# First attention of a two-block transformer kernel: rounds of two heads and two blocks of queries

## The chip, the cores and the metric

The kernel runs on one core of a Trainium2 chip. The metric is the device time of one execution in microseconds (us), as the median of several runs. TensorE multiplies matrices, VectorE (DVE in the profile) and ScalarE (ACT) work elementwise, GpSimd (POOL) does further elementwise work, and SyncE (SP) issues most transfers. Each engine works through its own instructions in program order, and semaphores tie the engines together.

## The reference

The program computes two transformer blocks one after the other, on 2048 tokens of 1024 features, all in float32. The change touches the attention of the first block alone:

```python
q = (rms_norm(x_q, q_norm_g) @ w_uq).reshape(B, S, 4, 192)      # 4 heads: 128 features and 64 rotary ones
q_nope, q_rope = q[..., :128], apply_rope(q[..., 128:], cos, sin)
k_nope, v = split((rms_norm(x_kv, kv_norm_g) @ w_ukv).reshape(B, S, 4, 256))
def attend(qn, qr, pq):                                          # for each block of 128 queries
    s = (einsum('bqhd,bkhd->bhqk', qn, k_nope) + einsum('bqhr,bkr->bhqk', qr, k_rope)) * 192 ** -0.5
    mask = pq[:, None, :, None] >= positions[:, None, None, :]
    p = softmax(where(mask, s, neg), axis=-1)
    return einsum('bqhk,bkhd->bqhd', p, v)
y_a = attend(...) * silu(gate_a)
```

The mask compares positions that are data, so every block of queries is multiplied with all 2048 keys. The cosines and sines of the rotary part are computed from the positions too. What follows (a pooling branch, the output product with a layer norm, and the whole second block with sparse attention and a gated recurrence) is not touched.

## The kernel before

**Groups and units.** Tokens are worked in G = 4 groups of TB = 512, each of BG = 4 blocks of P = 128 queries. The keys and values of all groups are made first. Then each group g makes its queries, runs the first attention and the output product ("1out", `project_out`), and the next group starts. `mla_units(g)` lists 16 units of the attention, a unit u being one head h of one block i: the four heads of a block, then the next block. `mla_steps(g)` is the order in which TensorE and VectorE go through the steps of the units. It is written out by hand, and each engine takes its own part of each step from it.

**A unit.** Its 128 queries are cut into four pieces of QUAD = 32, and the keys into 16 blocks of 128, each of four quarters. The step "score" (lines 2490 to 2506) writes four PSUM banks, one for each piece r: 16 products of 32 queries with 512 keys from `q_nope`, then 16 from `q_rope`. In a bank each 32 partitions hold the same queries with other keys. VectorE adds the mask, takes the maximum and writes `probs_1[n % 2]` (line 1862, four instructions), combines the maxima to biases (`bias_of`, lines 1741 to 1747), and writes one quarter of the next block's mask (`mask_of`, line 1733). ScalarE takes the four exponentials in place, with their sums (line 1430). In the step "turn" VectorE transposes them in squares of 32 (line 1876, four instructions) into `turned_1`, which is a view of `lat`, the buffer of the queries' latents. It waits before it until the value product of the unit before has been done (`pv_done`). In the step "value" TensorE multiplies 16 blocks of values (128 keys by 128 features) with `turned_1[:, k, :]`, 128 moving columns each, and adds up in a quarter of the bank `o_acc[i % 2]`.

**The order around it.** TensorE runs score(u), then value(u - 1). Once per block come "sums" (a small product that adds up the sums of the exponentials, line 2521, then a reciprocal), "share" (a product that spreads the reciprocals over the features, line 2527) and "blend" (VectorE multiplies with the gate and with `o_acc` into `y_all`, lines 1894 and 1898, and counts `y1_made`). Scores, sums and shares claim six banks in turn (`claim`, `drains`).

**Beside it.** GpSimd adds pairs of weight tiles and stores them during the attention of groups 0 and 1 (lines 1174 to 1177), and adds up parts of `y_all` once two of a group's four blends are done (`y1_made` at `BG * g + 2`). The positions of the keys lie as float32 in `pos_k`, which `rope_args` reads ahead of each group's queries (line 1667). After it ScalarE computes the tables (line 1295). Every f32 product shows as two MATMUL and two LDWEIGHTS records in the profile.

## Time and profile before

| what | value |
|---|---|
| runs: median (lowest to highest) | 3543.56 us (3541.99 to 3544.79) |
| the profiled execution: its time | 3533.97 us |
| its span, first to last instruction | 3532.0 us |
| mean granted TensorE clock | 0.969 |
| busy in the span: TensorE, VectorE, ScalarE, GpSimd | 94%, 59%, 38%, 20% |
| value products of the first attention (L2514) | 2048 records, 251.7 us busy |
| score products (L2497 and L2504) | 4096 records, 233.0 and 124.6 us busy |

A row of a group or of the timeline gives start and duration in us, engine, line, operation, what is written and read, the number of instructions (x32) and in brackets the idle time of the engine before them and what ended it. Matmuls overlap each other in a pipeline, so the time from one group's start to the next group's start says more than the durations. The granted clock is a share of TensorE's full 2.4 GHz, so 0.50 is its lower level of 1.2 GHz.

### The profile page before, as it was taken

What the parts mean: (1) busy time and instruction counts of PE and PEld (TensorE: products, weight loads), DVE (VectorE), ACT (ScalarE), POOL (GpSimd) and SP (SyncE); (2) the same over time, 40 slices, a digit from 0 to 9 for tenths busy, and PEclk for the clock granted to TensorE, in tenths of its full rate; (3) what the DMA queues carried; (4) which work ended last, traced back from release to release, by engine and by line L of the source; (5) the groups of instructions that cost most, each with busy time, mean ns of one, the idle gap of its engine ahead of it and who ended that gap; (6) DMA issues with size and microseconds to landing.
All of it is one profiled execution on the core that took longest, in us unless ns stands there. A gap on an engine that the chain in (4) does not pass through costs nothing.

```text
span 3532.0 us, 49781 instructions
## 1 busy us (share of the span) xinstructions
PE 3319.1 (94%) x18464; PEld 2044.8 (58%) x18464; DVE 2066.5 (59%) x4970; ACT 1358.4 (38%) x2595; POOL 706.4 (20%) x1093
## 2 busy tenths in 40 slices
PE   8999999999999999999989999899998898998887
PEld 3444577567656755745567455674555673545656
DVE  4417734773475457435563587835768635878653
ACT  2212312222222313132341465515775514786552
POOL 0016032112101210111121101312351111352011
PEclk9999999999999999989989999999999999998999
DMA  5226135304501420341204211041210041110004
GB/s 192 72 66 245 49 113 167 114 13 125 161 2 50 148 78 1 91 159 54 63 25 146 71 61 33 25 143 60 66 45 1 25 152 54 51 57 1 1 3 129
DMA packets 114159, 275.22 MB, mean 78 GB/s; under 512 B 11096, under 2 KB 12672, under 8 KB 111872
## 3 DMA queue, kind: packets, MB, share of 16 engines
q1 hardware_dynamic: 105584, 256.31, 22.8%
q10 hardware_dynamic: 8336, 15.74, 1.3%
q8 instruction: 148, 2.42, 0.3%
q14 instruction: 91, 0.75, 0.1%
HBM read 239.75 MB, written 32.26 MB: 77 GB/s over the span
## 4 chain that ended last, share of the span: by engine, by line
PE 78%; DVE 10%; ACT 6%; issue 5%; POOL 1%; DMA 0%; SPq 0%; ACTq 0%; DVEq 0%; POOLq 0%
PE bank L2342 24%; PE bank L2356 17%; PE o_acc L2514 6%; PE bank L2497 6%; PE bank L2744 3%; PE bank L2631 3%; PE bank L2504 3%; PE bank L2663 3%; PE bank L2756 2%; PE o_acc L2770 2%; PE bank L2593 1%; ACT prob_t L1485 1%; DVE tmp L2048 1%; PE bank L2415 1%; ACT index L1628 1%
## 5 line engine op out<-in xcount | busy, mean ns | idle before, releaser
L2342 PE MATMUL bank<-group_even,weights 128*128 128x512 f32 x1152 | 507.6, 598 | 11.2 <-DMA group_even<-in_x_t 5.8
L2342 PE MATMUL bank<-group_odd,weights 128*128 128x512 f32 x960 | 426.7, 600 | 6.2 <-ACT tmp L1471 6.2
L2342 PEld LDWEIGHTS bank<-group_even,weights 128*128 128x128 f32 x1152 | 218.4, 192 | 275.5 <-issue 275.3
L1430 ACT ACTIVATE probs<-probs,stat 128x512 f32<-128x512 f32 x256 | 181.7, 711 | 431.6 <-DVE stat L1747 431.6
L2342 PEld LDWEIGHTS bank<-group_odd,weights 128*128 128x128 f32 x960 | 181.9, 192 | 225.6 <-issue 225.2
L2514 PEld LDWEIGHTS o_acc<-lat,val 128*128 128x128 f32 x2048 | 242.2, 197 | 49.4 <-issue 41.4
L2514 PE MATMUL o_acc<-lat,val 128*128 128x128 f32 x2048 | 251.7, 283 | 12.9 <-DVE lat L1876 12.9
L2497 PE MATMUL bank<-k_nope,q_nope 128*32 128x512 f32 x2048 | 233.0, 595 | 0.0
L1862 DVE CUSTOM_DVE_ANT_0 probs<-bank,mask 128x512 f32<-128x512 f32 x256 | 161.4, 686 | 98.4 <-PE bank L2504 98.4
L2744 PE MATMUL bank<-kh,qa 64*128 64x512 f32 (+3 forms) x816 | 171.1, 501 | 16.0 <-DVE o_sb L2300 7.5
L1876 DVE STREAM_TRANSPOSE lat<-probs 128x512 f32<-128x512 f32 x256 | 168.8, 695 | 20.1 <-ACT probs L1430 20.0
L2356 PE MATMUL bank<-y_all,weights 128*128 128x256 f32 x768 | 172.4, 379 | 1.8 <-issue 1.8
L1619 ACT ACTIVATE prob_t<-bank 128x512 f32<-128x512 f32 (+3 forms) x240 | 116.6, 535 | 137.8 <-PE bank L2756 137.6
L2356 PEld LDWEIGHTS bank<-y_all,weights 128*128 128x128 f32 x768 | 145.6, 190 | 23.6 <-issue 4.1
L2770 PE MATMUL o_acc<-prob_t,v 128*64 128x128 f32 x1680 | 146.2, 282 | 10.7 <-ACT prob_t L1619 6.9
L2770 PEld LDWEIGHTS o_acc<-prob_t,v 128*64 128x64 f32 x1680 | 118.5, 139 | 56.7 <-issue 43.2
L2497 PEld LDWEIGHTS bank<-k_nope,q_nope 128*32 128x32 f32 x2048 | 60.0, 109 | 128.0 <-issue 118.2
L1144 POOL TENSOR_TENSOR y_all<-probs 128x512 f32<-128x512 f32 x32 | 33.4, 1045 | 492.5 <-DVE probs L1979 288.9
L2504 PE MATMUL bank<-k_rope,q_rope 64*32 64x512 f32 x2048 | 124.6, 595 | 0.0
L2744 PEld LDWEIGHTS bank<-kh,qa 64*128 64x128 f32 x816 | 79.2, 198 | 70.1 <-issue 38.7
L2048 DVE TENSOR_SCALAR_CACHE_REDUCE tmp<-index,mids 128x384 uint8<-128x384 f32 (+4 forms) x144 | 98.2, 719 | 11.1 <-POOL mids L1162 10.3
L2756 PE MATMUL bank<-ident,index 128*128 128x128 f32 x514 | 77.2, 292 | 23.7 <-ACT index L1628 21.6
(472 smaller groups left out, 6159.3 us busy)
## 6 DMA issues: line engine op xcount, KB each, us to landing
weights<-in_w_in SPq DMA_DIRECT2D x101, 512.0 KB, 3.6
weights<-w_sums SPq DMA_DIRECT2D x200, 256.0 KB, 3.3
weights<-in_w_out SPq DMA_DIRECT2D x96, 256.0 KB, 3.7
weights<-in_w_in_q SPq DMA_DIRECT2D x28, 512.0 KB, 3.6
weights<-in_w_in_q SPq DMA_DIRECT2D x54, 256.0 KB, 3.3
w_sums<-group_odd SPq DMA_DIRECT2D x10, 1024.0 KB, 4.6
weights<-in_w_i SPq DMA_DIRECT2D x20, 512.0 KB, 3.6
group_odd<-in_x_t SPq DMA_DIRECT2D x8, 1024.0 KB, 8.5
```

The source lines that it names most:

```text
L1430: A_(p, p, ACT.Exp, scale=QK_DIM ** -0.5, bias=stat[:, 16 + PARTS * (n % 2) + r:17 + PARTS * (n % 2) + r], accum_out=sums_1[:, i % 2, PART ...
L1862: drains(V.tensor_tensor_reduce(out=probs_1[n % 2][:, r * TB:(r + 1) * TB], in0=bank("score", i, h, r)[:], in1=mask[:, i % 2, r * TB:(r + ...
L1876: V.transpose(turned_1[:, :, r * QUAD:(r + 1) * QUAD], probs_1[n % 2][:, r * TB:(r + 1) * TB].rearrange("p (k q) -> p k q", k=NB)).then_in ...
L2048: V.tensor_scalar(tested_dve[:, b, 0:n], index_of(BG * g + b)[:, 0:n], mids[:, b, r:r + 1], 0.0, ALU.is_ge, ALU.add, accum_out=counts[:, b ...
L2342: ins = M(bank(*name)[:], ring[n % SLOTS][:, k * P:(k + 1) * P], rhs[:, k, :], start=(k == 0), stop=(k == chunks - 1))
L2356: ins = M(bank(*name)[:, 0:HALF], ring[n % SLOTS][:, at % 2 * TB + k * P:at % 2 * TB + (k + 1) * P], of[:, k, :], start=(OPENED_BY[m] == m ...
L2497: M(bank("score", i, h, r)[c * QUAD:(c + 1) * QUAD, :].rearrange("p (k n) -> p k n", n=QUAD), q_nope[:, h, b * P + r * QUAD:b * P + (r + 1 ...
L2504: ins = M(bank("score", i, h, r)[c * QUAD:(c + 1) * QUAD, :].rearrange("p (k n) -> p k n", n=QUAD), q_rope[half, h, at:at + QUAD], keys[:, ...
L2514: ins = M(o_acc[i % 2][:, h * P:(h + 1) * P], val[:, k, h * P:(h + 1) * P], turned_1[:, k, :], start=(h == 0 and k == 0), stop=(h == H1 - ...
L2744: ins = M(bank("s2", i, 2 * p + e, c)[:, at:at + end - first], qa[rows, p, (i % BG) * P:(i % BG + 1) * P], kh[rows, a, p, first:end], star ...
L2756: ins = nc.tensor.transpose(bank("p2_t", i, h, c)[:, (k % BG) * P:(k % BG + 1) * P], probs_of(g, u, e)[:, k * P:(k + 1) * P], ident[:])
L2770: ins = M(o_acc[i % 2][e * DH2:(e + 1) * DH2, p * P:(p + 1) * P], v2[:, k, h * DH2:(h + 1) * DH2], prob_slots[2 * (m % 2) + e][:, (k % BG) ...
```

## The change

A round is now two heads of two blocks, ROUND = 4 units. `mla_units` goes through a pair of blocks head by head, so that two units in a row have the same head. The values of the two are multiplied at once: the transposes of both units fill one buffer `turned_` of 16 x 256 columns, and a "value" step is made after every second unit, with 256 moving columns for each block of values and half a bank of `o_acc`. The transposes of an even unit wait until the value product of the pair before has been done; those of an odd unit wait for no product. Sums, share and blend are made once per round, as often as before. The mask quarters of a whole block are written in one go, in the units 0, 7, 8 and 15 of a group.

`turned_` takes the place of `lat` and `pos_k`. As the first attention now overwrites the positions, ScalarE loads 512 of them into `o_sb` at the end of each group but the last, after the last blend, and VectorE converts them to float32 ahead of `rope_args`.

```diff
--- before.py
+++ after.py
@@ -67,24 +67,30 @@
 PARTS = P // QUAD
 
 
+
+
+ROUND = 4
+
+
 def mla_units(g):
 
-    return [(BG * g + b, h) for b in range(BG) for h in range(H1)]
+    return [(BG * g + 2 * pair + b, h) for pair in range(BG // 2) for h in range(H1) for b in range(2)]
 
 
 def mla_steps(g):
 
     units = mla_units(g)
     for u, (i, h) in enumerate(units):
+        r = BG * g + u // ROUND
         yield ("score", u)
-        if u > 0:
-            if h == 0:
-                yield ("sums", i - 1)
-            if h == 1 and i % BG > 0:
-                yield from [("share", i - 1), ("blend", i - 1)]
-            yield ("value", u - 1)
+        if u > 0 and u % 2 == 0:
+            if u % ROUND == 0:
+                yield ("sums", r - 1)
+            if u % ROUND == 2 and u > ROUND:
+                yield from [("share", r - 1), ("blend", r - 1)]
+            yield ("value", u // 2 - 1)
         yield ("turn", u)
-    yield from [("sums", i), ("value", u), ("share", i), ("blend", i)]
+    yield from [("sums", r), ("value", u // 2), ("share", r), ("blend", r)]
 
 
 def mla_tiles(g):
@@ -588,12 +594,14 @@
         val = alloc(one, "val", [P, NB, TB])
         q_nope = alloc(one, "q_nope", [P, H1, TB])
         q_rope = alloc(one, "q_rope", [P, H1, TB // 2])
-        lat = alloc(one, "lat", [P, 4, TB])
+        turned_ = alloc(one, "turned", [P, NB, 2 * P])
+        lat = turned_[:, 0:NB // 2, :].rearrange("p k q -> p (k q)").rearrange("p (j t) -> p j t", j=4)
+        pos_k = turned_[:, NB // 2:, :].rearrange("p k q -> p (k q)")
         turns = alloc(one, "turns", [P, 2, TB])
         cos, sin = turns[:, 0, :], turns[:, 1, :]
-        pos_k = alloc(one, "pos_k", [P, S])
         pos_i = probs[:, 0:S].bitcast(i32)
         pos_k4, pos_k4_i = prob_t[:, 2, :], probs[:, S:S + TB].bitcast(i32)
+        pos_g = o_sb[:].bitcast(i32)
         pos_q = alloc(one, "pos_q", [P, NB * PARTS])
         pos_qi = probs[:, S + TB:S + TB + NB * PARTS].bitcast(i32)
         same = alloc(one, "same", [P, P])
@@ -640,7 +648,6 @@
         decay = alloc(two, "decay", [P, 2, BG])
         two.close()
         probs_1 = probs[:, 0:S], probs[:, S:2 * S]
-        turned_1 = lat[:, :, :].rearrange("p j t -> p (j t)").rearrange("p (k q) -> p k q", k=NB)
         spread_1 = prob_t[:, 0, :].rearrange("p (n q) -> p n q", q=QUAD)
         sums_1 = stat[:, 32:64].rearrange("p (a n) -> p a n", a=2)
         mask_i = probs[:, S:S + KC * P].bitcast(i32)
@@ -772,6 +779,7 @@
         dve_step = sem("dve_step")
         pool_step = sem("pool_step")
         rope_arg = sem("rope_arg")
+        pos_here = sem("pos_here")
         rope_made = sem("rope_made")
         k_normed = sem("k_normed")
         q_normed = sem("q_normed")
@@ -1427,8 +1435,12 @@
                         act.wait_ge(row_max, PARTS * (n + 1))
                         for r in range(PARTS):
                             p = probs_1[n % 2][:, r * TB:(r + 1) * TB]
+                            at = PARTS * (u % ROUND) + r
                             A_(p, p, ACT.Exp, scale=QK_DIM ** -0.5, bias=stat[:, 16 + PARTS * (n % 2) + r:17 + PARTS * (n % 2) + r],
-                               accum_out=sums_1[:, i % 2, PARTS * h + r:PARTS * h + r + 1]).then_inc(probs_made, 1)
+                               accum_out=sums_1[:, u // ROUND % 2, at:at + 1]).then_inc(probs_made, 1)
+                if g + 1 < G:
+                    act.wait_ge(y1_made, BG * (g + 1))
+                    act.dma_start(pos_g, A["pos_k"][:, (g + 1) * TB:(g + 2) * TB].broadcast_to([P, TB])).then_inc(pos_here, 16)
 
             second_begins(act)
             act.wait_ge(t5_made, 1)
@@ -1664,7 +1676,12 @@
                     dve.wait_ge(rope_made, n)
                 ang, turn = tmp[:, 0, :], tmp[:, 1, :]
                 fr = VEC["inv_freq"]
-                step(dve, V.tensor_scalar(ang, pos_k[:, g * TB:(g + 1) * TB], vec[:, fr:fr + 1], None, ALU.mult))
+                at = pos_k[:, g * TB:(g + 1) * TB]
+                if n > G:
+                    dve.wait_ge(pos_here, 16 * (n - G))
+                    step(dve, V.tensor_copy(ang, pos_g))
+                    at = ang
+                step(dve, V.tensor_scalar(ang, at, vec[:, fr:fr + 1], None, ALU.mult))
                 step(dve, V.tensor_scalar(turn, ang, 1.0 / TWO_PI, 12582912.0, ALU.mult, ALU.add))
                 step(dve, V.tensor_scalar(turn, turn, 12582912.0, None, ALU.subtract))
                 for c in (C1, C2, C3):
@@ -1710,7 +1727,7 @@
 
             dve.wait_ge(vec_here, 16)
             dve.wait_ge(const_here, 16 * 7)
-            step(dve, V.tensor_copy(pos_k[:], pos_i))
+            step(dve, V.tensor_copy(pos_k, pos_i))
             step(dve, V.tensor_copy(pos_q[:], pos_qi))
             step(dve, V.tensor_copy(pos_k4, pos_k4_i))
             for c in range(PARTS):
@@ -1754,7 +1771,7 @@
 
             def scale_queries(g):
 
-                V.tensor_tensor(lat[:], lat[:], wide(rstd, 4), ALU.mult).then_inc(q_normed, 1)
+                V.tensor_tensor(lat, lat, wide(rstd, 4), ALU.mult).then_inc(q_normed, 1)
 
             def pool_window(g, j):
 
@@ -1865,15 +1882,18 @@
                         for r in range(PARTS):
                             wait_drained(dve, "score", i, h, r)
                         bias_of(n)
-                        mask_of(i + 1, h)
+                        if u % (2 * ROUND) in (0, 2 * ROUND - 1):
+                            for r in range(PARTS):
+                                mask_of(i + 1, r)
                     elif kind == "turn":
                         u = st[1]
                         n = unit_no(g, u)
-                        if n > 0:
-                            dve.wait_ge(pv_done, n)
+                        if u % 2 == 0 and n > 0:
+                            dve.wait_ge(pv_done, n // 2)
                         for r in range(PARTS):
                             dve.wait_ge(probs_made, PARTS * n + r + 1)
-                            V.transpose(turned_1[:, :, r * QUAD:(r + 1) * QUAD],
+                            at = (u % 2) * P + r * QUAD
+                            V.transpose(turned_[:, :, at:at + QUAD],
                                         probs_1[n % 2][:, r * TB:(r + 1) * TB].rearrange("p (k q) -> p k q", k=NB)).then_inc(turned, 1)
                     elif kind == "sums":
                         i = st[1]
@@ -1888,14 +1908,15 @@
                                                op1=ALU.mult).then_inc(inverse_made, 1)
                     elif kind == "blend":
                         i = st[1]
-                        at = (i % BG) * P
+                        heads = slice(2 * (i % 2), 2 * (i % 2) + 2)
+                        tokens = slice(i % BG // 2 * 2 * P, (i % BG // 2 + 1) * 2 * P)
                         wait_tile(dve, "share1_t", i)
-                        share = o_sb[:].rearrange("p (h t) -> p h t", h=H1)
-                        drains(V.tensor_tensor(share, bank("share1_t", i)[:].rearrange("p (h t) -> p h t", h=H1),
-                                               gate[:, :, at:at + P], ALU.mult), "share1_t", i)
+                        share = o_sb[:].rearrange("p (h t) -> p h t", h=2)
+                        drains(V.tensor_tensor(share, bank("share1_t", i)[:].rearrange("p (h t) -> p h t", h=2),
+                                               gate[:, heads, tokens], ALU.mult), "share1_t", i)
                         wait_drained(dve, "share1_t", i)
-                        dve.wait_ge(pv_done, H1 * (i + 1))
-                        V.tensor_tensor(y_of(g)[:, 0:H1, at:at + P], o_acc[i % 2][:].rearrange("p (h t) -> p h t", h=H1), share,
+                        dve.wait_ge(pv_done, 2 * (i + 1))
+                        V.tensor_tensor(y_of(g)[:, heads, tokens], o_acc[i % 2][:].rearrange("p (h t) -> p h t", h=2), share,
                                         ALU.mult).then_inc(y1_made, 1)
 
                 late_sum("1", g, dve, V)
@@ -2505,14 +2526,15 @@
                                         q_rope[half, h, at:at + QUAD], keys[:, c], start=False, stop=True)
                             ins.then_inc(tile_ready, 1)
                     elif kind == "value":
-                        u = st[1]
-                        i, h = units[u]
-                        if h == 0 and i >= 2:
-                            pe.wait_ge(y1_made, i - 1)
+                        u = 2 * st[1] + 1
+                        h = units[u][1]
+                        r, e = BG * g + u // ROUND, u % ROUND // 2
+                        if e == 0 and r >= 2:
+                            pe.wait_ge(y1_made, r - 1)
                         pe.wait_ge(turned, PARTS * (unit_no(g, u) + 1))
                         for k in range(NB):
-                            ins = M(o_acc[i % 2][:, h * P:(h + 1) * P], val[:, k, h * P:(h + 1) * P], turned_1[:, k, :],
-                                    start=(h == 0 and k == 0), stop=(h == H1 - 1 and k == NB - 1), skip_group_check=True)
+                            ins = M(o_acc[r % 2][:, e * 2 * P:(e + 1) * 2 * P], val[:, k, h * P:(h + 1) * P], turned_[:, k, :],
+                                    start=(e == 0 and k == 0), stop=(e == 1 and k == NB - 1), skip_group_check=True)
                         ins.then_inc(pv_done, 1)
                     elif kind == "sums":
                         i = st[1]
```

## Rows read from the trace of the kernel before

**Rows 1.** The page's first part: busy time of each engine and share of the span

```profile
PE 3319.1 (94%) x18464; PEld 2044.8 (58%) x18464; DVE 2066.5 (59%) x4970; ACT 1358.4 (38%) x2595; POOL 706.4 (20%) x1093
```

**Rows 2.** Timeline of TensorE in group 2: start, duration in us, line, count

```profile
1056.38 3.84 PE L2514 MATMUL o_acc<-lat,val 128*128 128x128 f32 x32
1060.15 3.64 PE L2497 MATMUL bank<-k_nope,q_nope 128*32 128x512 f32 x32
...
1065.60 3.84 PE L2514 MATMUL o_acc<-lat,val 128*128 128x128 f32 x32
...
1074.82 0.40 PE L2521 MATMUL bank<-stat,same 128*128 128x16 f32 x2
...
1084.26 1.12 PE L2527 MATMUL bank<-prob_t,ones 128*128 128x512 f32 x2
1085.22 3.73 PE L2514 MATMUL o_acc<-lat,val 128*128 128x128 f32 x32
```

**Rows 3.** Timeline at the end of group 3, all engines

```profile
1434.41 0.69 DVE L1862 CUSTOM_DVE_ANT_0 probs<-bank,mask 128x512 f32<-128x512 f32 x1 [1.55 <-PE bank L2504]
...
1435.16 3.84 PE L2514 MATMUL o_acc<-lat,val 128*128 128x128 f32 x32
...
1438.40 0.72 ACT L1430 ACTIVATE probs<-probs,stat 128x512 f32<-128x512 f32 x1 [6.29 <-DVE stat L1747]
...
1441.39 0.40 PE L2521 MATMUL bank<-stat,same 128*128 128x16 f32 x2 [2.39 <-ACT probs L1430]
...
1442.13 5.47 PE L2514 MATMUL o_acc<-lat,val 128*128 128x128 f32 x32 [0.35 <-DVE lat L1876]
```

**Rows 4.** Timeline of products with 256 moving columns in group 1's output

```profile
819.90 1.89 PE L2356 MATMUL bank<-gate,weights 128*128 128x256 f32 x8
...
821.63 1.89 PE L2356 MATMUL bank<-turns,weights 128*128 128x256 f32 x8
```

**Rows 5.** Timeline at the head of group 3

```profile
1290.09 3.64 PE L2497 MATMUL bank<-k_nope,q_nope 128*32 128x512 f32 x32
...
1299.09 0.49 DVE L1733 TENSOR_SCALAR mask<-prob_t,pos_q 128x512 bf16<-128x512 f32 x1
...
1302.91 1.35 PE L2514 MATMUL o_acc<-lat,val 128*128 128x128 f32 x10 [1.85 <-DVE lat L1876]
```

**Rows 6.** Timeline of VectorE, groups 0 and 1: masks, stretched steps, transposes

```profile
285.84 2.05 DVE L1733 TENSOR_SCALAR mask<-prob_t,pos_q 128x512 bf16<-128x512 f32 x4
...
309.23 0.69 DVE L1862 CUSTOM_DVE_ANT_0 probs<-bank,mask 128x512 f32<-128x512 f32 x1 [2.05 <-PE bank L2504]
...
316.89 0.49 DVE L1733 TENSOR_SCALAR mask<-prob_t,pos_q 128x512 bf16<-128x512 f32 x1
...
638.26 2.27 DVE L1742 SCALAR_TENSOR_TENSOR stat<-stat 64x4 f32<-64x4 f32 x1
...
718.36 2.48 DVE L1876 STREAM_TRANSPOSE lat<-probs 128x512 f32<-128x512 f32 x4
```

**Rows 7.** First value products of groups 0, 1; waits in group 0 (total, times, longest)

```profile
299.13 5.47 PE L2514 MATMUL o_acc<-lat,val 128*128 128x128 f32 x32 [3.10 <-DVE lat L1876]
...
635.47 6.59 PE L2514 MATMUL o_acc<-lat,val 128*128 128x128 f32 x32 [3.50 <-DVE lat L1876]
...
PE o_acc L2514 <- DVE lat L1876: 4.8, 3, 3.1
```

**Rows 8.** A stretch of group 1: busy us, granted clock (PEclk), DMA

```profile
636.00:638.00 2.00, 2.00 (x12) 2.00 (x11) 1.86 (x7) 0.00 (x0) 1.92 (x2) 0.50 0.00 0
```

**Rows 9.** Timeline of TensorE after a long wait in the second block

```profile
2943.22 9.83 PE L2342 MATMUL bank<-group_odd,weights 128*128 128x512 f32 x16 [6.21 <-ACT tmp L1471]
```

**Rows 10.** Timeline where the rotary tables of group 2 are made

```profile
831.99 7.03 PE L2342 MATMUL bank<-group_even,weights 128*128 128x512 f32 x16
...
832.52 0.48 DVE L1667 TENSOR_SCALAR tmp<-pos_k,vec 128x512 f32<-128x512 f32 x1
...
839.72 0.63 ACT L1295 ACTIVATE turns<-turns 128x512 f32<-128x512 f32 x1 [61.75 <-DVE turns L1679]
```

## The prediction

> **What bounds the kernel now.** I began with the page: TensorE is busy for 94% of the span and VectorE for 59% [rows 1], so time is won or lost where TensorE's own work or a wait of TensorE changes. The change touches one stage, the first attention, which runs four times (groups 0 to 3 of 16 units, a unit being one head of one block of 128 queries). I then read TensorE's timeline inside a group. A unit starts every 9.22 us (1056.38 to 1065.60): the value product takes 3.77 us (to 1060.15) and the score products the other 5.45 [rows 2]. Nothing waits there. Once per block come the product of the sums, 0.22 us more (9.44 instead of 9.22), and that of the shares, 0.96 us before the value product starts [rows 2].
>
> Last I read the end of group 3, because there TensorE runs out of cover and the chain through the other engines stands bare [rows 3]. The scores of unit 15 end at 1435.16, where the value product of unit 14 starts. VectorE had begun to take them at 1434.41; it forms maxima and biases, ScalarE's exponentials start at 1438.40, the four transposes follow them, and the value product of unit 15 starts at 1442.13. **From the end of a unit's scores to the earliest start of its value product are 6.97 us.** (The same difference stands at each of the four group ends; one is shown.) Inside a group TensorE has 3.77 + 5.45 = 9.22 us of other work in that time, so the chain is hidden with 2.25 us to spare. This slack is what the change spends.
>
> **The change part by part.**
>
> *The value product.* 32 records of 128 columns for a unit become 32 of 256 columns for two units. Other f32 products of 256 columns start 8 records in 1.73 us (819.90 to 821.63), 0.216 us each [rows 4]: 32 make 6.9, and I take 6.95. Before, two units took 2 x 3.77 = 7.54. TensorE's own work falls by 0.59 us for each of the 32 pairs, 19 us in all, if nothing waits. (The Trainium skill, "TensorE: Matmul & The Clock Gate", section "Back-to-back issue gap", gives N/2.4 + 2.5 ns per matmul at the full clock, so 56 and 109 ns; by that a pair would save only 64 x 56 - 32 x 109 ns = 0.1 us, 3 us in all. The rows have 0.118 and 0.216 us per f32 record, so they leave more to gain and decide.)
>
> *The order.* After the change TensorE runs: scores of the odd unit, scores of the next even unit, value product of the pair. Between the end of the odd unit's scores and its value product lie 5.45 us of cover where 6.97 are wanted [rows 2, 3]. TensorE waits 1.52 us in every pair inside a group. The next odd unit's scores can only follow the value product in program order, so a pair lasts 5.45 + 6.97 + 6.95 = 19.37 us, against 18.44. The products of sums and shares now fall into the wait and are free: the one wants the exponentials, which are ready 6.23 us after the scores (1441.39) [rows 3]. VectorE's other work of an even unit is hidden too: its maxima and biases last from 6.9 to 10.9 us after the odd scores' end, and its transposes must wait anyway until the value product ends at 13.9, since the pair's one buffer is still being read. Up to 3 us of masks, sums or blending fit in between. Behind that wait the next reduce stands in VectorE's queue, which has work only from 18.6 on; the transposes end at 16.5. So the new wait on the whole value product costs nothing more.
>
> *One group without disturbance* (group 3 is the pattern, and group 2 has the same head within 0.2 us). Before: first value product 12.82 us after the first score (1290.09 to 1302.91) [rows 5], last one 139.22 us later (1442.13), then 3.77: 155.8 us. After, the head is longer, since the first product needs two chains one behind the other. Unit 0's biases are done at 9.0 (1299.09) [rows 5]; four masks instead of one take 2.05, four transposes without a wait 2.48 [rows 6]: 13.5. Then unit 1's chain from its first reduce to the product, 1434.41 to 1442.13, is 7.7 [rows 3]: 21.2 us, while TensorE, done with three scores at 16.35, idles 4.8. Seven pairs follow, 7 x 19.37 = 135.6, then 6.95. Units 7 and 15 carry four masks between bias and transposes. 2.05 + 2.48 us there, against 3.73 from the first exponential to the product (1438.40 to 1442.13), makes 0.86 more with the 0.06 of the handover; group 3 has that once, the others twice. Sum: 164.6 us for group 3 and 165.5 for the others. That is 8.8 + 3 x 9.7 = **+38 us**.
>
> *GpSimd beside VectorE.* In group 0 the small bias steps stretch while GpSimd adds weights: from first reduce to mask unit 2 took 7.66 us (309.23 to 316.89) [rows 6], where group 3 needs 4.0 (1434.41 to 1438.40, the same point) [rows 3]. The stretch is 0.1 to 3.7 us in the six units that overlap GpSimd's work, 1.2 on the mean. Before, most of it was hidden. Three odd units (1, 3, 5) now expose it, 3.6 us, less the 1.3 that group 0 waited already beside its 3.1 at the head and 0.4 at the end [rows 7]; unit 1 of group 1 adds 2.1 (one step of some 0.15 us took 2.27 there) [rows 6]. Together **+4**.
>
> *The clock.* Before, the waits of 3.10 and 3.50 us ahead of the first value product of groups 0 and 1 were followed by value products of 5.47 and 6.59 us instead of 3.84 [rows 7], with a granted clock of 0.50, the 1.2 GHz level [rows 8]. The waits of 1.85 us at group 3's head [rows 5] and of 1.3 in group 0 were not. Two of the four group ends lost 1.6 us likewise (1442.13, 5.47 us) [rows 3]. These losses, 1.6 + 2.8 + 2 x 1.6 = 7.6 us, lie in the time before and not in my clean 155.8, so **-8**. After the change every group has two long idles: 4.8 us at its head and 6.2 at its end (up to the sums). A wait of 6.21 us elsewhere cost 2.8 us (16 records in 9.83 us, against 7.03) [rows 9, 10]. From 1.6 to 3.0 each, I take 2.3 for eight, **+18**. (The Trainium skill, same page, section "Why this matters for your kernels", warns of idle gaps between bursts because the clock falls back; these rows agree. It speaks against this change.)
>
> *The positions.* Three times, at the end of groups 0 to 2, ScalarE waits for the last blend and issues one load of 256 KB, and VectorE converts 512 columns before the rotary tables. ScalarE is then idle for 61.75 us before its next work, which is what stands behind the wait in its queue; the tables begin at 832.52, some 50 us after group 1's end at 783; TensorE is in a 7 us product at that time [rows 10]. Load and conversion are covered. Bare, the conversions would cost 0.4 to 0.7 us each, 2 at most. The mask writes are the same number; SyncE's and GpSimd's queues get nothing new.
>
> *Sum*: 38 + 4 - 8 + 18 = +52, and 1 for the conversions and small handovers: **+53 us**. The profiled execution took 3533.97 us (span 3532.0), which would become 3587; the median of the runs is 3543.56, 0.27% above it, and I add the same 53 to that: **3596.6 us**.
>
> **Rivals.**
>
> *TensorE sets the pace (faster).* If the chain were hidden behind 5.45 us of scores and the groups' edges were no longer than now, only the 32 x 0.59 us would be left: 3524.6. It decides at a chain of 5.45 us. For it: TensorE waits only 4.8 us in group 0 now, in three places [rows 7], so the chain has always had cover. Against it: the bare 6.97 at four group ends, of which nothing in the edit makes any step shorter. The single mask that leaves the odd units lies beside the exponentials. Chance 0.05.
>
> *Cheap waits (no change).* Should the wait inside the groups vanish but the edges stay as reckoned, it is 24 x 1.52 = 36 us less (six of a group's eight value products lie inside): 3560, and 3542, so within 0.2%, if the edges keep their clock. Chance 0.03.
>
> *The clock falls inside the groups too.* The idles inside are 0.6 to 1.3 us, after sums or shares, and waits of 1.3 to 1.85 did not lower it; but a stretched chain in groups 0 and 1 makes idles of 2 to 4 us. If each of 24 pairs lost 1.6 us: +38, 3635; a few of them, +5 to 10. Chance 0.10 for a part or all.
>
> *The edges keep the clock.* Without the 18 it is 3579. For it: two of four group ends did not lose it before. Against it: the idles are two to three times as long now. It is inside the forecast's range.
>
> **How the numbers follow.** Forecast 0.82, by itself 3580 to 3612: clock 8 x 1.6 to 8 x 3.0 us, contention 0 to 11, value product 6.9 to 7.05. The range 3574 to 3616 takes in edges at full clock and some interior clock loss, and leaves out the faster case and a clock that falls everywhere. 0.2% is 7 us, about what a measurement of this kernel can tell from no change. Slower 0.92, same 0.03, faster 0.05.
>
> **What the profile after will show.** Value products of 256 columns, 1024 records, about 6.95 us per pair; pairs of 19.4 us; waits of TensorE of 0.5 to 1.3 us before the 24 value products inside the groups, 4.8 us at each head and 6.2 at each end; VectorE waiting for the value product before the even transposes; the first value product some 21 us into a group; the mean granted clock lower than 0.969. The forecast is wrong if the distance from an odd unit's last score to its value product is not 6.97 us, if a 256-column record takes other than 0.216 us, or if the half clock turns up within the groups.

## The result

The changed kernel takes 3608.87 us (median of 4 runs, 3605.82 to 3610.23), against 3542.77 us for the kernel before in the same comparison. The ratio is 1.0188, with a 95% interval of 1.0171 to 1.0206: 66 us slower. The forecast was 53 us more, and a range of 3574 to 3616. The profiled execution took 3605.82 us (span 3603.8), 71.8 more than the span before.

The first part of the page and the rows of its groups that answer to [rows 1] and to the value product:

```profile
PE 3328.8 (92%) x17440; PEld 2012.8 (56%) x17440; DVE 2068.4 (57%) x4973; ACT 1358.7 (38%) x2595; POOL 706.5 (20%) x1093
...
L2536 PE MATMUL o_acc<-turned,val 128*128 128x256 f32 x1024 | 254.6, 411 | 32.4 <-DVE turned L1896 32.3
...
L1896 DVE STREAM_TRANSPOSE turned<-probs 128x512 f32<-128x512 f32 x256 | 167.8, 692 | 93.0 <-PE o_acc L2536 70.5
```

There are 1024 records of 256 columns. TensorE waits 32.3 us ahead of them for VectorE's transposes, and VectorE waits 70.5 us ahead of its transposes for the value product, a wait that the profile before does not have.

TensorE's timeline in group 2 (start, duration, line, count, idle before and its cause), which answers to [rows 2]:

```profile
1034.64 0.40 PE L2543 MATMUL bank<-stat,same 128*128 128x16 f32 x2 [0.70 <-ACT probs L1439]
1035.38 7.17 PE L2536 MATMUL o_acc<-turned,val 128*128 128x256 f32 x32 [0.35 <-DVE turned L1896]
1042.49 3.64 PE L2518 MATMUL bank<-k_nope,q_nope 128*32 128x512 f32 x32
...
1047.94 3.64 PE L2518 MATMUL bank<-k_nope,q_nope 128*32 128x512 f32 x32
...
1053.39 1.12 PE L2549 MATMUL bank<-prob_t,ones 128*128 128x512 f32 x2
1055.00 7.14 PE L2536 MATMUL o_acc<-turned,val 128*128 128x256 f32 x32 [0.49 <-DVE turned L1896]
1062.08 3.64 PE L2518 MATMUL bank<-k_nope,q_nope 128*32 128x512 f32 x32
...
1067.52 3.64 PE L2518 MATMUL bank<-k_nope,q_nope 128*32 128x512 f32 x32
...
1073.76 0.40 PE L2543 MATMUL bank<-stat,same 128*128 128x16 f32 x2 [0.71 <-ACT probs L1439]
1075.40 2.83 PE L2536 MATMUL o_acc<-turned,val 128*128 128x256 f32 x6 [1.25 <-DVE turned L1896]
```

A value product ends, the odd unit's scores follow (1042.49), then the even unit's (1047.94), and the next value product starts 7.06 us after the odd unit's scores ended. With the product of the shares in the wait the next value product starts 19.62 us after this one (1035.38 to 1055.00), with the product of the sums 19.50 us (1096.70 to 1116.20, further on in the group); two units took 18.44 before. The fourth value product (1075.40) starts 7.88 us after the scores' end, because four mask writes stand before its transposes. It also ran slowly, 8.79 us instead of 7.08: the granted clock (PEclk, the third number from the end, before the DMA share and GB/s) is 0.57 in its first part and 1.00 again from 1080 on.

```profile
1075.00:1079.00 4.00, 3.60 (x9) 2.85 (x10) 3.70 (x15) 0.00 (x0) 0.00 (x0) 0.57 0.00 0
1080.00:1084.00 4.00, 4.00 (x20) 3.42 (x18) 2.15 (x5) 2.15 (x7) 0.00 (x0) 1.00 0.01 2
```

Here is VectorE beside it, in the even unit (the first row is the last of its small steps before the transposes):

```profile
1081.60 0.69 DVE L1906 SCALAR_TENSOR_TENSOR prob_t<-same,inverse 128x512 f32<-128x512 f32 x1
...
1084.30 2.49 DVE L1896 STREAM_TRANSPOSE turned<-probs 128x512 f32<-128x512 f32 x4 [2.00 <-PE o_acc L2536]
...
1088.89 0.69 DVE L1879 CUSTOM_DVE_ANT_0 probs<-bank,mask 128x512 f32<-128x512 f32 x1 [2.10 <-PE bank L2525]
...
1093.73 2.83 DVE L1896 STREAM_TRANSPOSE turned<-probs 128x512 f32<-128x512 f32 x4 [0.88 <-ACT probs L1439]
...
1096.70 1.53 PE L2536 MATMUL o_acc<-turned,val 128*128 128x256 f32 x6 [0.49 <-DVE turned L1896]
```

The transposes of the even unit wait 2.00 us for the value product, and after them VectorE waits another 2.10 us for the next scores, so the even unit's wait delays nothing. The odd unit's chain runs from 1088.89 to 1096.70, 7.81 us, in which VectorE waits only for the exponentials (0.88 us), and TensorE stands at its end.

The end of group 3, which answers to [rows 3]:

```profile
1502.74 0.61 PE L2543 MATMUL bank<-stat,same 128*128 128x16 f32 x2 [6.15 <-ACT probs L1439]
1503.48 9.89 PE L2536 MATMUL o_acc<-turned,val 128*128 128x256 f32 x32
1513.21 1.02 PE L2549 MATMUL bank<-prob_t,ones 128*128 128x512 f32 x2
```

TensorE is idle for 6.15 us there, where it was 2.39 [rows 3], and the last value product occupies 9.73 us, where one at full clock occupies 7.08.

**Where the 66 us are.** I measured each group of the attention from its first score product to the product of the shares behind its last value product. The third row is the changed kernel's time from the first score to the first value product.

| group | 0 | 1 | 2 | 3 | sum |
|---|---|---|---|---|---|
| before, us | 160.0 | 161.8 | 155.5 | 157.3 | 634.7 |
| after, us | 182.2 | 175.7 | 172.3 | 171.8 | 702.0 |
| first value product after, us | 25.1 | 24.6 | 21.1 | 21.1 | |

That is 67.3 us (the sums are of unrounded times). Each of the three stretches between the groups takes 175.9 us in both kernels. The rest of the two spans' difference lies at the start (1.5 us less) and behind the first attention: 2084.6 us in the profile before, 2090.6 after, and 2088.0 to 2093.8 in all other profiles of this study. One execution of the kernel before stands out low there, and its runs go from 3533 to 3549 us; so kernels are compared by their ratios.

### The profile page after: what moved, and what is told of

It reads as the page before. It is cut to its first block, busy times and chain, and to the rows that moved or that the text cites. A ratio compares the mean times of both kernels' runs of the same rounds, so it can differ in the third digit from the quotient of the medians.

```text
span 3603.8 us, 47699 instructions
## 1 busy us (share of the span) xinstructions
PE 3328.8 (92%) x17440; PEld 2012.8 (56%) x17440; DVE 2068.4 (57%) x4973; ACT 1358.7 (38%) x2595; POOL 706.5 (20%) x1093
## 4 chain that ended last, share of the span: by engine, by line
PE 71%; DVE 15%; ACT 6%; issue 5%; POOL 1%; DMA 0%; SPq 0%; ACTq 0%; DVEq 0%; POOLq 0%
PE bank L2363 23%; PE bank L2377 17%; PE o_acc L2536 7%; PE bank L2518 3%; PE bank L2766 3%; PE bank L2653 3%; DVE turned L1896 3%; PE bank L2685 3%; PE bank L2778 2%; PE o_acc L2792 2%; DVE probs L1879 2%; PE bank L2615 1%; ACT prob_t L1497 1%; PE bank L2525 1%; DVE tmp L2069 1%
## 5 line engine op out<-in xcount | busy, mean ns | idle before, releaser
L2536 PE MATMUL o_acc<-turned,val 128*128 128x256 f32 x1024 | 254.6, 411 | 32.4 <-DVE turned L1896 32.3
L2536 PEld LDWEIGHTS o_acc<-turned,val 128*128 128x128 f32 x1024 | 209.8, 208 | 79.5 <-issue 28.7
L1896 DVE STREAM_TRANSPOSE turned<-probs 128x512 f32<-128x512 f32 x256 | 167.8, 692 | 93.0 <-PE o_acc L2536 70.5
L2792 PE MATMUL o_acc<-prob_t,v 128*64 128x128 f32 x1680 | 147.1, 284 | 10.1 <-ACT prob_t L1631 6.3
```

What stands on the lines that cost most here:

```text
L1896: V.transpose(turned_[:, :, at:at + QUAD], probs_1[n % 2][:, r * TB:(r + 1) * TB].rearrange("p (k q) -> p k q", k=NB)).then_inc(turned, 1)
L2536: ins = M(o_acc[r % 2][:, e * 2 * P:(e + 1) * 2 * P], val[:, k, h * P:(h + 1) * P], turned_[:, k, :], start=(e == 0 and k == 0), stop=(e = ...
L2792: ins = M(o_acc[i % 2][e * DH2:(e + 1) * DH2, p * P:(p + 1) * P], v2[:, k, h * DH2:(h + 1) * DH2], prob_slots[2 * (m % 2) + e][:, (k % BG) ...
```

## The experiments

Each ratio is taken to the kernel before on the same chip; "attention" is the sum of the four groups as above, from the one profiled execution of each kernel. The kernel before has 634.7 there.

| kernel | median us | ratio (95% interval) | attention us |
|---|---|---|---|
| changed | 3608.87 | 1.0188 (1.0171 to 1.0206) | 702.0 |
| e1_narrow | 3614.96 | 1.0211 (1.0195 to 1.0227) | 705.5 |
| e2_halves | 3559.00 | 1.0050 (1.0032 to 1.0068) | 649.1 |
| e7_no_reload | 3606.00 | 1.0186 (1.0171 to 1.0202) | 702.3 |
| e3_masks | 3593.35 | 1.0153 (1.0134 to 1.0172) | 688.8 |
| e4_warm | 3591.63 | 1.0144 (1.0127 to 1.0160) | 685.9 |
| e5_ahead | 3580.66 | 1.0111 (1.0095 to 1.0126) | 675.9 |
| e6_mixed | 3548.22 | 1.0018 (1.0009 to 1.0028) | 641.9 |
| e8_mixed_warm | 3540.03 | 0.9998 (0.9989 to 1.0007) | 639.7 |
| e9_wide_late_warm | 3537.19 | 0.9988 (0.9978 to 0.9997) | 629.7 |
| e11_wide_late | 3542.55 | 0.9998 (0.9989 to 1.0007) | 635.6 |
| e10_before_warm | 3532.22 | 0.9977 (0.9968 to 0.9986) | 628.3 |

### Is it the wide product, or its wait?

e1_narrow keeps all of the change but the width:

```diff
-for k in range(NB):
-    M(o_acc[r % 2][:, e * 2 * P:(e + 1) * 2 * P], val[:, k, ...], turned_[:, k, :], ...)
+for b in range(2):
+    for k in range(NB):
+        M(o_acc[r % 2][:, (2 * e + b) * P:(2 * e + b + 1) * P], val[:, k, ...], turned_[:, k, b * P:(b + 1) * P], ...)
```

> The changed kernel, with each pair's value product as two runs of 128 moving columns instead of one of 256; both still wait for the transposes of both units. Exposed chain: the waits stay and the product grows from the 7.08 us seen in the trace to the 7.54 of before, so 32 x 0.46 = 15 us slower than the changed kernel, near 3624. If the 256-column product itself were what costs: near 3543 to 3560, the waits gone.

Measured: 0.23% above the changed kernel by the ratios, 8 us (4 in the attention, as nine value products ran slowly instead of 13). The wait stays, so the wide product is not what costs; but it brings less than I reckoned. A pair of group 2:

```profile
1119.32 7.41 PE L2537 MATMUL o_acc<-turned,val 128*128 128x128 f32 x64 [0.35 <-DVE turned L1896]
1126.66 3.64 PE L2518 MATMUL bank<-k_nope,q_nope 128*32 128x512 f32 x32
```

64 narrow records behind each other occupy 7.34 us, 32 wide ones 7.1 (1035.38 to 1042.49). The width saves 0.24 us per pair, 8 us in all. The 7.54 us of before are another 0.2 us longer; there the same 64 records are started in two runs.

e2_halves puts the narrow products in their old places, each behind the scores of the next unit, waiting for its own transposes only:

```diff
+        if u > 0:
+            yield ("half", u - 1)
...
-            yield ("value", u // 2 - 1)
```

> The changed kernel, with 128 columns and each unit's product in its old place, after the next unit's scores, waiting only for its own transposes; the order of units, the rounds, the mask bursts and the reloaded positions stay. Exposed chain: 9.22 us of cover again, so about the time before and some 6 us for masks in the head and in unit 15: near 3549. If order, masks, rounds or the reload cost by themselves: 3580 or more.

Measured: ratio 1.0050. Of the changed kernel's 1.88% all but 0.5% is gone, with rounds, order, masks and reload in place, so it is the place of the product behind its transposes that costs. The rest was expected at 6 us and is 14 in the attention. The heads and the ends of three groups, where the mask bursts stand, make 6 of it (first value products at 15.7, 14.8, 13.5 and 13.5 us against 14.1, 14.5, 12.6 and 12.8; last ones 7.9 us after the scores' end against 6.97). Behind the longer waits the value products are slow more often, which I had left out: first products of 5.4 us in groups 2 and 3 (3.7 before), last ones of 5.3 to 6.6 in all four.

e7_no_reload drops the three loads and conversions, and with them the right rotary tables of groups 1 to 3:

> The changed kernel without the three loads of positions and their conversions; the rotary tables of groups 1 to 3 are computed from what the transposes left there, so this part of the computation is left out. Covered reload: within 2 us of the changed kernel, 3607 to 3609. If the reload or ScalarE's wait for the last blend costs: 3590 or less.

Measured: 1.0186 against 1.0188, no difference. In the changed kernel's trace the load is issued at 819.86 and its conversion runs at 867.10, so there are 47 us between them.

```profile
819.86 0.34 ACTq L1443 DMA_DIRECT2D o_sb<-in_pos_k  x1
...
867.10 0.42 DVE L1682 CAST tmp<-o_sb 128x512 f32<-128x512 int32 x1
```

### Which parts of the exposed time?

e3_masks moves the mask writes into places where VectorE waits anyway:

```diff
-if u % (2 * ROUND) in (0, 2 * ROUND - 1):
-    for r in range(PARTS): mask_of(i + 1, r)
+if u % (2 * ROUND) == 2 * ROUND - 2:
+    for r in range(PARTS): mask_of(i + 2, r)
+if u == 2 * ROUND:
+    for r in range(PARTS): mask_of(i + 1, r)
...
+for r in range(PARTS): mask_of(BG * g + 1, r)      # ahead of unit 0
```

> The changed kernel, with the masks moved off the exposed chain: the even block's in unit 6 and 14 instead of 7 and 15, the odd block's ahead of unit 0. Exposed chain and clock: 0.9 us less at unit 7 in four groups and at 15 in three, the 1.7 us of half clock after unit 7 gone in four, 0.8 to 1.4 less at four heads: 16 us less, near 3593. If only the 0.9 us counts and the clock falls anyway: 9 us less. If masks are hidden: no change, 3609.

Measured: 12 us less by the ratios, 13 in the attention and 15.5 by the medians, where 16 were expected with the clock counted and 9 without it. In groups 1 to 3 the fourth value products start 19.5 us after the third instead of 20.4, and in all four they occupy 7.1 us instead of 8.8. Groups 2 and 3 gain 5.1 and 3.9 us, groups 0 and 1 only 3.0 and 1.1; in these, other products are slower than in the changed kernel, such as the first one of group 1 (10.1 us instead of 8.6).

e4_warm fills TensorE's waits at the head and the end of each group, ahead of the fourth value product and in one place of group 0 with products that nothing uses (called idle products below). At the end of a group:

```diff
+if i % BG == BG - 1 or i == 0:
+    for _ in range(13 if i % BG else 6):
+        M(o_acc[i % 2][:, 2 * P:4 * P], ones[:], k_nope[:, 0, 0:2 * P], start=True, stop=True, ...)
 pe.wait_ge(probs_made, PARTS * H1 * (i + 1))
```

> The changed kernel, with idle products (ones by keys, 256 columns, into a part of the accumulator that is written anew afterwards) put into TensorE's waits at each group's head, before the fourth value product, at each end, and in one stretched wait of group 0. The clock as a cost of the waits: most of the 25 us that the trace shows at half clock come back, 15 to 22 us less than the changed kernel, 3587 to 3594. If the slow value products have another cause: no change or a few us more, 3609 to 3614.

Measured: 1.0144, 16 us below the changed kernel by the ratios and in the attention alike (702.0 to 685.9). In groups 1 to 3 every value product is at full speed. The end of group 3:

```profile
1483.21 5.88 PE L2549 MATMUL o_acc<-k_nope,ones 128*128 128x256 f32 x26
1489.43 0.40 PE L2552 MATMUL bank<-stat,same 128*128 128x16 f32 x2 [0.34 <-ACT probs L1439]
1490.18 7.17 PE L2542 MATMUL o_acc<-turned,val 128*128 128x256 f32 x32 [0.35 <-DVE turned L1896]
```

Unit 15's chain takes the 6.97 us that it took before (1483.21 to 1490.18), and the product behind it lasts 7.17 us where it lasted 9.89. The waits themselves therefore cost part of the time, and the clock after them another part. Two products of group 0 stay slow, behind waits of 3.00 and 4.12 us that the idle products did not cover.

e5_ahead moves the first quarter of the next odd unit's scores ahead of the value product:

```diff
+if begun != u + 2 and u + 2 < len(units):
+    begun = u + 2
+    nope_scores(*units[begun], 0)
 pe.wait_ge(turned, PARTS * (unit_no(g, u) + 1))
```

> The changed kernel, with the first quarter of the next odd unit's first score products (0.91 us) moved ahead of each value product, so that TensorE has 6.4 us of cover instead of 5.45. Exposed chain: every pair inside a group 0.7 to 0.9 us shorter, 22 us in all, and up to 7 more where the clock no longer falls at the fourth product: 3580 to 3587. If the waits are not what costs: 3609.

Measured: 1.0111, 27 us less by the ratios, 26 in the attention. In group 2:

```profile
1080.82 7.17 PE L2546 MATMUL o_acc<-turned,val 128*128 128x256 f32 x32
...
1097.96 1.06 PE L2517 MATMUL bank<-k_nope,q_nope 128*32 128x512 f32 x8
1098.95 0.39 PE L2556 MATMUL bank<-stat,same 128*128 128x16 f32 x2
1099.48 7.17 PE L2546 MATMUL o_acc<-turned,val 128*128 128x256 f32 x32
```

No wait over 0.14 us is left there, and the pair lasts 18.66 us instead of 19.50. With the shares in it a pair lasts 19.2 instead of 19.6. This is the same work in another order: 0.9 us of cover per pair is worth 26 us, and 9 of them are clock, by what the value products occupy beyond 7.08 us in either kernel.

### Can the wide product pay?

e6_mixed joins what the others showed: narrow products in the old places for the first and the last pair of a group, wide ones with the quarter of scores ahead for the six between, and the masks of e3.

> A version meant to beat both: 256 columns for the six inner pairs with the quarter of scores ahead, 128 columns in the old places for the first and the last pair, masks off the chain. Exposed chain: edges as before the change, each inner pair 18.7 to 18.9 us against 18.4 and half of the 1.1 for sums and shares before: 1 us less per group than before the change, 3538 to 3543 where the kernel before has 3543. If rounds and order cost by themselves: over 3555.

Measured: 1.0018, 6 us slower than before, where 0 to 5 less was expected. Groups 1 to 3 take 159.2, 155.3 and 155.3 us, 5 us less than before in sum; group 0 takes 172.1 instead of 160.0. TensorE there:

```profile
348.07 1.07 PE L2525 MATMUL bank<-k_nope,q_nope 128*32 128x512 f32 x8
353.67 9.91 PE L2567 MATMUL o_acc<-turned,val 128*128 128x256 f32 x32 [4.53 <-DVE turned L1904]
363.51 2.78 PE L2525 MATMUL bank<-k_nope,q_nope 128*32 128x512 f32 x24
```

Of the chain 4.53 us have no cover, and the product behind the wait is slow again. VectorE and GpSimd in that chain:

```profile
345.13 4.78 DVE L1767 TENSOR_TENSOR stat<-stat 32x4 f32<-32x4 f32 x4
346.31 1.27 POOL L1188 TENSOR_TENSOR group_odd<-group_odd 128x512 f32<-128x512 f32 x1
347.54 2.35 POOL L1214 TENSOR_TENSOR roots<-y_all 128x1024 f32<-128x1024 f32 x1
```

Four bias steps take 4.78 us there, and 0.71 in the units that run without GpSimd. That GpSimd's work causes the stretch is read from such rows; no run takes it away.

e8_mixed_warm adds idle products to the waits at each head and end:

> The one before, with idle products of 128 columns in the waits at each group's head (1.4 us) and end (1.8 us). If they keep the clock up there: 5 to 8 us less than without them, 3531 to 3537. If not: the same as without, within 2 us.

Measured: 0.9998, 0.2% less than without, and level with the kernel before. The attention accounts for 2 of these 7 us (639.7 against 641.9); the profiles differ by another 5 us behind the attention, in a part that both share. So the 5 to 8 us that were expected are not shown to come from the clock. Group 0 still takes 170.2 us.

e9_wide_late_warm and e11_wide_late keep the narrow products through the first eight units of group 0, with and without the idle products:

> The version with 128 columns at the edges, 256 inside and idle products in the waits, but in group 0, whose first eight units overlap GpSimd's weight sums, these units too keep 128 columns in the old places. If the tie of that version with the kernel before came from group 0 alone (170.2 us there against 160.0 before, while the others are 157 to 159 against 155.5 to 161.8): 10 us less, near 3530. If the rest of the program pays instead: 3540.

> The first of these three without idle products: 10 to 12 us less than the mixed version with wide products from the second pair of group 0 on (3548), so near 3537, as the kernel before or a few us less.

Measured: 0.9988 and 0.9998. Group 0 falls to 160.3 and 163.6 us, so e6's loss against the kernel before was there. By the ratios this brings 0.1 to 0.2% where 0.3 were expected; the attention fell by 10 and 6 us.

e10_before_warm is the kernel before with the idle products alone:

> The kernel before, with the same idle products at the head (1.4 us) and the end (1.8 us) of each group. If the clock that its own waits cost comes back: 4 to 7 us less than the kernel before, 3534 to 3537. If not: 3541. What the last one has beyond this is the gain of the wide products.

Measured: 0.9977, 8 us faster than the kernel before and the fastest of all; 6.4 of them are in the attention. Its last value products occupy 3.67 us in every group (5.31 in two of them before) and its first ones 3.77 (5.4 and 6.5 in groups 0 and 1 before):

```profile
1432.72 1.95 PE L2524 MATMUL o_acc<-k_nope,ones 128*128 128x128 f32 x16
1435.27 0.39 PE L2527 MATMUL bank<-stat,same 128*128 128x16 f32 x2 [0.60 <-ACT probs L1430]
1436.02 3.84 PE L2517 MATMUL o_acc<-lat,val 128*128 128x128 f32 x32 [0.35 <-DVE lat L1876]
```

So the gain of e9 over the kernel before is not that of the wide products. With the idle products in both, the mixed order takes 155.2 and 155.2 us in groups 2 and 3, the old order 155.5 and 155.7, and in sum 629.7 against 628.3: the wide product gains nothing that this kernel's measurement can tell.

## Why the prediction was right, and where it was short

**The mechanism held.** A chain of 6.97 us behind the odd unit's scores, with 5.45 us of cover, was the main step. It measures 6.97 to 7.06 us inside the groups, and 7.88 with the masks (6.97 and 0.86 were reckoned to make 7.83). e2 and e5 show that it decides: give the chain its cover back and the time returns. Sums and shares fell into the wait, as said, and the even unit's wait for the value product cost nothing (2.10 us of slack behind it). The heads came out at 21.1 us in groups 2 and 3 against 21.2 forecast. One detail of them was not foreseen: TensorE stops in the middle of unit 2's scores for a bank, 1.20 us in group 2, because VectorE has not yet taken unit 1's scores. So the 4.8 us of idle time came as two waits of 1.20 and 3.25 us; the first value product was not delayed by the first of them, as it still waited 3.25 us for its transposes. The reload was covered (e7).

**The sizes.** The attention grew by 67 us where my sum had 53, and the time came out inside the range because its top lay 19 us above the forecast. These terms make the difference (52 without the 1 for the conversions, and 15 more); hardly any error cancelled another:

| term | forecast, us | measured, us |
|---|---|---|
| wide product of a pair | 6.95 | 7.08 to 7.11, so 4 more over 32 pairs |
| chain inside the groups | 6.97 | up to 7.06, 1 more |
| GpSimd beside VectorE, net of before | 4 | 6 |
| half clock at heads and ends | 18 | 17 (eight products, 1.5 to 2.8 each) |
| half clock inside the groups | 0 | 9 (five products, 1.7 each) |

The measured GpSimd term: the heads of groups 0 and 1 are 4.0 and 3.5 us longer than those of groups 2 and 3, and the second value product of group 0 came 9.9 us after the scores' end instead of 6.97, which makes 10.5; the kernel before had 4.4 of the same kind. The stretch falls on other pairs from kernel to kernel: in e7's profile it is the third pair of group 0 that waits long (3.96 us), with the same 182 us for the group. The clock terms are what each value product occupied beyond 7.08 us.

**The step that was short** is that of the clock, and in it the sentence on the idles inside the groups, "0.6 to 1.3 us". I had put four masks before the transposes of unit 7 into the sum, 0.86 us, and did not carry them over to the idle time. With them TensorE is idle for 0.71 and then 1.25 us, and the clock fell in all four groups; the fifth slow product inside is the second one of group 0, behind a stretched chain (3.67 us of idle time), as the rival had it for the early groups. I had that case as a rival, at a chance of 0.10 for a part or all of it; a part came. e3 takes it away with the masks, e4 with idle products. The forecast of the eight edges was right in sum. So two of the prediction's own signs of being wrong turned up, half clock within the groups and a record of 0.221 us instead of 0.216, and cost 9 and 4 of the 66 us.

**Two slips in the working.** By its own terms (clock 8 x 1.6, no contention, value product 6.9) the lower end of the forecast is 3586, not 3580. And the 4.8 us that TensorE "waits only" in group 0 are those ahead of its value products; with the 2.39 us ahead of the sums it waits 7.2. Neither moves the 53 us.

**The gain was overstated.** The 0.59 us per pair came from comparing 0.216 us a record with 2 x 3.77 us. By the formula of the Trainium skill ("TensorE: Matmul & The Clock Gate", section "Back-to-back issue gap") the estimate was 0.1 us. The section calls it the gap of an isolated matmul, which under-counts at small N. The measured records of 0.115 and 0.221 us are about twice its 56 and 109 ns, so this trace does not bear it out for f32. The measurement, 0.24 us for the width alone, lies between the two. The rest of the 0.59 was the second run of products (0.2) and the wide one, set 0.15 us too short. This hardly touched the time, as TensorE was waiting; it matters for e6 to e11, where TensorE was at work and the wide product still paid nothing.

**What stays open.** Why the clock falls after some waits and not after others of the same length: the fourth value product is slow in four of four groups of the changed kernel and in one of four of e1 (7.3 us in the others), behind the same waits of 0.71 and 1.25 us. And e9 stands 0.11% above e10 while its attention is only 1.4 us longer; the rest of that lies in parts of the program that they share, within the scatter of the runs. That GpSimd causes the stretched bias steps is not tested by a run. Two buffers for the transposes were not tried.

## What to carry to other kernels

Before a product is put behind the transposes of two units instead of one, read the bare chain where the pipeline drains (here 6.97 us at a group's end) and compare it with the cover that the new order leaves (5.45 us), not with the busy shares: the difference is paid once per product, and the edges, where no other product covers it, pay the whole chain. Mind also that a chain is not always of its shortest length: an order with 2 us of slack absorbs most of what another engine's work does to it, one without slack pays each time. And a wait of TensorE can cost twice, once as itself and once in the clock of what follows, so filling unavoidable waits with products that nobody reads is a cheap thing to try: it gave 8 us to the kernel before, and no other version here was faster than that.

## What the runs showed of the hardware

- The granted clock fell to the 1.2 GHz level after two waits of 0.71 and 1.25 us with a small product between them, in four of four groups of the changed kernel; before, a wait of 1.85 us had not lowered it [rows 5]. In group 2 it was 1.00 up to 1075, in the waits, 0.77 in the next microsecond, in which the value product starts, and 0.50 from 1076 to 1078. Each time it cost 1.7 us; after the idles of 6.15 us at the ends it cost 2.2 to 2.7 us. A chain of such waits does not always lower it: in e1 it did so in one group of four.
- Products into an accumulator that is written anew afterwards kept the clock up: 26 records of 5.88 us in a wait, and the value product behind them lasted 7.17 us instead of 9.89, at a granted clock of 1.00 (1490 to 1497) where it had been 0.50 (1503 to 1507).
- A value product with 256 columns per record is 3% shorter than the same work with 128 (7.1 against 7.34 us), each f32 record taking 0.221 and 0.115 us.
- Small VectorE steps stretched while GpSimd worked: four bias steps of 0.71 us together took 4.78 (e6, 345.13) and 2.80 us (changed kernel, 302.14).
